# An encoder block on one core: conditioning sums by POOL products and accumulating DMAs, values split once, four mixer passes written out

## The reference

```
c_act = silu(c)
mod = c_act @ w_ada + b_ada          # (6*1024): sh1, sc1, g1, sh2, sc2, g2
h = rms_norm(x, norm1_gain) * (1 + sc1) + sh1
x = x + g1 * token_mixer(h, ...)
h = rms_norm(x, norm2_gain) * (1 + sc2) + sh2
x = x + g2 * conv_ffn(h, ...)
# token_mixer: one input projection to B, C, u | q, k, v | g_A, g_B
y_a = B * dwconv3(C * u)
y_b = windowed attention (|t-s| <= 128, 16 query heads, 4 key/value heads, ALiBi, sink)
merged = sigmoid(g_A) * y_a + sigmoid(g_B) * y_b ; out = merged @ w_o
```

## Time and profile before

| | us |
|---|---|
| median of 3 runs (870.09 to 871.1) | 870.67 |
| span of the profiled execution | 870.4 |
| the four mixer passes in it (72.5 to 168.3, 260.6, 350.4, 441.8) | 95.8, 92.3, 89.8, 91.4 |
| PE busy over the span | 799.9 (92%) |
| DVE busy over the span | 615.6 (71%) |
| POOL busy over the span | 377.8 (43%) |

### The profile page before, as it was taken

The page is one execution under the profiler, slowest core; times in us unless marked ns, Lnnn a source line. Parts: engine busy times, 40 slices in busy tenths (PEclk is TensorE's granted clock), DMA queues, the critical chain, the costliest instruction groups (busy, mean ns, idle before and its releaser), DMA issues.

```text
span 870.4 us, 11305 instructions
## 1 busy us (share of the span) xinstructions
PE 799.9 (92%) x3753; PEld 656.6 (75%) x3753; DVE 615.6 (71%) x781; ACT 349.3 (40%) x589; POOL 377.8 (43%) x170
## 2 busy tenths in 40 slices
PE   3579699998999899979999899999999999999997
PEld 2468577877777777867778788888888888887886
DVE  5969899598959996898753788888888888200000
ACT  5326245454345444534542454444444443122220
POOL 3824342443325243422494434555555555445341
PEclk9679799998999999999999999999999999999999
DMA  9813612362134413541123132232222322223311
GB/s 329 303 49 131 208 57 90 117 200 69 52 140 155 134 48 99 188 146 48 48 78 116 49 98 96 96 96 96 96 96 96 96 96 84 97 85 108 120 37 48
DMA packets 79726, 95.79 MB, mean 110 GB/s; under 512 B 2210, under 2 KB 71002, under 8 KB 79706
## 3 DMA queue, kind: packets, MB, share of 16 engines
q1 hardware_dynamic: 75482, 93.43, 32.2%
q10 hardware_dynamic: 4224, 2.10, 0.8%
HBM read 93.43 MB, written 2.10 MB: 110 GB/s over the span
## 4 chain that ended last, share of the span: by engine, by line
PE 64%; DVE 22%; issue 9%; DMA 3%; ACT 1%; DVEq 1%; SPq 0%; ACTq 0%
PE bank L652 20%; PE bank L654 20%; PE bank L653 20%; DVE acc L1083 2%; DVE a_buf L1173 2%; DVE prob L1124 2%; DMA ada<-in_w_ada_dram 2%; DVE sm L1140 1%; DVE acc L996 1%; DVE sm L1131 1%; PE bank L791 1%; PE bank L775 1%; DVE prob L1143 1%; DVE q_st L1096 1%; DVE pt_lo L1149 1%
## 5 line engine op out<-in xcount | busy, mean ns | idle before, releaser
L341 POOL TENSOR_TENSOR w_lo<-w_raw,w_hi 128x1024 fp32r<-128x1024 f32 x127 | 333.5, 2645 | 432.7 <-ACT w_hi L415 432.7
L652 PE MATMUL bank<-h_hi,w_hi 128*128 128x512 f32 (+1 forms) x792 | 310.5, 392 | 5.5 <-DVE h_lo L1317 4.3
L653 PE MATMUL bank<-h_lo,w_hi 128*128 128x512 f32 (+1 forms) x792 | 307.0, 388 | 0.0
L654 PE MATMUL bank<-h_hi,w_lo 128*128 128x512 f32 (+1 forms) x792 | 306.7, 387 | 0.0
L652 PEld LDWEIGHTS bank<-h_hi,w_hi 128*128 128x128 f32 x792 | 151.2, 191 | 36.2 <-DVE h_lo L1317 4.0
L654 PEld LDWEIGHTS bank<-h_hi,w_lo 128*128 128x128 f32 x792 | 151.0, 191 | 30.4
L653 PEld LDWEIGHTS bank<-h_lo,w_hi 128*128 128x128 f32 x792 | 151.1, 191 | 28.5
L415 ACT ACTIVATE w_hi<-w_raw 128x1024 fp32r<-128x1024 f32 x128 | 128.7, 1051 | 108.6 <-PE bank L654 102.0
L654 PE MATMUL bank<-g_hi,w_lo 128*128 128x512 f32 x176 | 70.0, 398 | 0.0
L652 PE MATMUL bank<-g_hi,w_hi 128*128 128x512 f32 x176 | 69.9, 397 | 0.0
L653 PE MATMUL bank<-g_lo,w_hi 128*128 128x512 f32 x176 | 69.3, 394 | 0.0
(11 more groups left out here) (175 smaller groups left out, 1076.5 us busy)
## 6 DMA issues: line engine op xcount, KB each, us to landing
w_raw<-in_w_in_dram SPq DMA_DIRECT2D x26, 1024.0 KB, 5.1
ada<-in_w_ada_dram SPq DMA_DIRECT2D x48, 512.0 KB, 6.0
w_raw<-in_w_up_dram SPq DMA_DIRECT2D x22, 1024.0 KB, 5.1
w_raw<-in_w_down_dram SPq DMA_DIRECT2D x8, 1024.0 KB, 4.9
w_raw<-in_w_o_dram SPq DMA_DIRECT2D x4, 1024.0 KB, 5.0
w_raw<-in_w_down_dram SPq DMA_DIRECT2D x4, 768.0 KB, 4.2
x_nat<-in_x_dram SPq DMA_DIRECT2D x4, 512.0 KB, 4.9
out_dram<-b_buf ACTq DMA_DIRECT2D x4, 256.0 KB, 2.3
```

What stands on the lines that cost most here:

```text
L341: pool.tensor_tensor(w_lo[:, n % 2, u], w_raw[:, n % 2, :, u * P:(u + 1) * P], w_hi[:, n % 2, u], SUB).then_inc(lo_ready, 1)
L652: pe.matmul(dst, w_h, rhs_hi, start=first, stop=False)
L653: pe.matmul(dst, w_h, rhs_lo, start=False, stop=False)
L654: return pe.matmul(dst, w_l, rhs_hi, start=False, stop=last)
```

## The change

The four passes are written out (`for g in range(KV)`) on all engines instead of looped. `v_nat` goes: ACT copies the high part of the values of all four heads straight from PSUM to a larger `v_st`, and DVE subtracts the low part, once, ahead of the passes. `gemv` leaves DVE. POOL makes each product of row block k in place (k = 0 goes straight to `acc`), and for k = 1 to 7 issues a DMA that adds the row to `acc` in SBUF; a DMA waits for the one before it. The steps stand one between the two halves of `low` and one behind. PE's `ada_turn` moves from slots 13 and 17 to slots 22 and 23, and DVE's `ada_sums` with it. SP's loads of `ada` now wait for a product or an accumulation instead of `gemv_done`; those of k = 0 and 1 for the last pass's `ada_turn` (`mod_done`).

```diff
-        v_nat = sb("v_nat", [P, NB, KV * HD], into=mixer)
-        v_st = sb("v_st", [P, NB, 2, HD], f32r, into=mixer)
+        v_st = sb("v_st", [P, NB, KV, 2, HD], f32r, into=mixer)
...
@@ sync
-                    for k in ([], [], [0, 1, 2, 3], [4, 5], [6, 7], [])[n]:
-                        sp.wait_ge(gemv_done, g * KT + (G0 + k - 1))
+                    for k in ([], [], [0, 1], [2, 3], [4, 5], [6, 7])[n]:
+                        if k < 2:
+                            sp.wait_ge(mod_done, g * 2 + 4)
+                        elif k == 2:
+                            sp.wait_ge(ada_scaled, g * KT + 1)
+                        else:
+                            sp.wait_ge(ada_added, g * (16 * (KT - 1)) + 16 * (k - 2))
...
@@ gpsimd
-            with pool.Fori(0, KV) as g:
+            for g in range(KV):
+                def ada_step(k):
+                    row = ada[:, k % 2, :]
+                    pool.wait_ge(ada_in[k % 2], g * (8 * KT) + (16 * (k // 2) + 16))
...
+                    pool.tensor_scalar(acc[:, :] if k == 0 else row, row, c_act[:, 0, k:k + 1], 1.0,
+                                       MUL, MUL).then_inc(ada_scaled, 1)
+                    if k == 0:
+                        return
+                    pool.wait_ge(ada_scaled, g * KT + (k + 1))
+                    if k > 1:
+                        pool.wait_ge(ada_added, g * (16 * (KT - 1)) + 16 * (k - 1))
+                    pool.dma_start(acc[:, :], row, accum_op=ADD).then_inc(ada_added, 16)
...
-                    low(g, NM, P_MIX + n + 1)
+                    low(g, NM, P_MIX + n + 1, (0,))
+                    if 1 <= n <= 4:
+                        ada_step(2 * n - 1)
+                    low(g, NM, P_MIX + n + 1, (1,))
+                    if n < 4:
+                        ada_step(2 * n)
@@ scalar
-            act.activation(v_nat[:, 2, :], bank[6][:, 0:PC], ACT.Copy).then_inc(o_free, 1)
+            for b in V_ORDER:
+                act.activation(v_st[:, b, :, 0, :], v_heads(b), ACT.Copy).then_inc(v_high, 1)
@@ tensor
-                    pe.wait_ge(gemv_done, g * KT + (G0 + KT))
+                    pe.wait_ge(ada_scaled, g * KT + KT)
+                    pe.wait_ge(ada_added, g * (16 * (KT - 1)) + 16 * (KT - 1))
...
-                    if slot in (13, 17):
-                        ada_turn((slot - 13) // 4)
+                    if slot in (22, 23):
+                        ada_turn(slot - 22)
@@ vector
-            for b, done in ((0, t_free), (1, t_free), (3, m_free)):
-                dve.tensor_copy(v_nat[:, b, :], bank[4 + b][:, 0:PC]).then_inc(done, 1)
+            for n, b in enumerate(V_ORDER):
+                dve.wait_ge(v_high, n + 1)
+                dve.tensor_tensor(v_st[:, b, :, 1, :], v_heads(b), v_st[:, b, :, 0, :],
+                                  SUB).then_inc((t_free, t_free, o_free, m_free)[b], 1)
...
-                gemv(0)
-                gemv(1)
-                stage_values()
                 query_low(0)
-                gemv(2)
-                gemv(3)
                 query_sums(0)
...
                 take(0, (0, 1))
-                gemv(4)
                 take(0, (2, 3))
-                gemv(5)
                 shift(0)
-                gemv(6)
-                gemv(7)
                 take(1, (0, 1))
```

More of the change, by code:

```diff
@@ L196, in encoder_block @@
         r_copy, xr_pool = sem("x_rstd_copied"), sem("x_normed_by_pool")
+        ada_scaled, ada_added = sem("ada_scaled"), sem("ada_added")
         cb_done, pe_ada, mod_read, amp_done = sem("c_spread"), sem("ada_used_by_pe"), sem("mod_read"), sem("amp_done")
@@ L231, in encoder_block, with v_heads @@
         WO_HALVES = [(0, 6, 6), (0, 7, 7), (1, 6, 4), (1, 7, 5)]
+        V_ORDER = (2, 3, 0, 1)
+        def v_heads(b):
+            return bank[4 + b][:, 0:PC].rearrange("p (j d) -> p j d", d=HD)
         def half(c):
@@ L262, in encoder_block @@
         NT = 10
-        STEPS, STEPS_UP = 36, 8
+        STEPS_UP = 8
         block = ctx.enter_context(nc.Block())
@@ L311, in _ @@
                     load(None, 0, 1, wi[:, :, COL_V:COL_V + PC])
-            with sp.Fori(1, KV + 1) as g1:
-                g = g1 - 1
+            for g in range(KV):
+                g1 = g + 1
                 for n in range(NM):
                     load(g, NM, P_MIX + n, wi[:, :, bass.ds(g1 * PC + (MIX[n] - PC), PC)])
-                    for k in ([], [], [0, 1, 2, 3], [4, 5], [6, 7], [])[n]:
-                        sp.wait_ge(gemv_done, g * KT + (G0 + k - 1))
+                    for k in ([], [], [0, 1], [2, 3], [4, 5], [6, 7])[n]:
[5 more added lines that the diff above has]
+                            sp.wait_ge(ada_added, g * (16 * (KT - 1)) + 16 * (k - 2))
                         sp.dma_start(ada[:, k % 2, :],
@@ L371, in _ @@
             low(None, 0, 2)
-            with pool.Fori(0, KV) as g:
+            pool.wait_ge(cb_done, 1)
+            for g in range(KV):
+                def ada_step(k):
+                    row = ada[:, k % 2, :]
+                    pool.wait_ge(ada_in[k % 2], g * (8 * KT) + (16 * (k // 2) + 16))
+                    if k == 0:
+                        pool.wait_ge(mod_done, g * 2 + 4)
+                    pool.tensor_scalar(acc[:, :] if k == 0 else row, row, c_act[:, 0, k:k + 1], 1.0,
+                                       MUL, MUL).then_inc(ada_scaled, 1)
+                    if k == 0:
+                        return
[3 more added lines that the diff above has]
+                    pool.dma_start(acc[:, :], row, accum_op=ADD).then_inc(ada_added, 16)
                 for n in range(NM):
@@ L468, in _ @@
                                    ACT.Copy).then_inc(kh_done, 1)
-            with act.Fori(0, KV) as g:
+            for g in range(KV):
                 U = 2 * P_MIX
@@ L729, in _ @@
                 mm.then_inc(kt_done, 1)
-            with pe.Fori(0, KV) as g:
+            for g in range(KV):
                 def unit_waits(n):
@@ L787, in values @@
                     last = i == len(TS[b]) - 1
-                    hi_lo = (bank[OB][:, :], v_st[:, kb], pt_hi[:, t % 2, :])
-                    hi = (bank[OB][0:HD, :], v_st[:, kb, 0, :], pt_lo[:, t % 2, :])
+                    hi_lo = (bank[OB][:, :], v_st[:, kb, g], pt_hi[:, t % 2, :])
+                    hi = (bank[OB][0:HD, :], v_st[:, kb, g, 0, :], pt_lo[:, t % 2, :])
                     for n, args in enumerate((hi, hi_lo) if last else (hi_lo, hi)):
@@ L1228, in _ @@
                 taps(1)
-                ada_sums(0)
                 conv_out(1)
@@ L1238, in _ @@
                 turned_low(TS[2][2:])
-                ada_sums(1)
                 normalise(3)
@@ L1243, in _ @@
                 turned_low(TS[3])
+                ada_sums(0)
                 heads_out(3)
+                ada_sums(1)
                 dve.wait_ge(m_free, g * 2 + 3)
@@ L1250, in _ @@
                 merge(1)
-                steps.leave(KV)
             steps.link(dve.scalar_tensor_tensor(amp[:, 1, :], mod[:, 4 * KT:5 * KT], 1.0, par[:, PA_G2:PA_G2 + KT],
```

3 lines of the change are left out of this document (1 added, 2 removed).

## The result

The changed kernel takes **890.9 us** (median of 4 runs, 880.4 to 902.2), beside 870.9 (870.1 to 874.8) for the kernel before. The ratio is 1.012 [1.0095, 1.0148], so the change makes the kernel slower, by 1.2%. The forecast was 841 (834 to 868) and faster. The time of the changed kernel is far more scattered than that of before; I read its profiled run, which took 884.5 us with a span of 882.7, against the span of 870.4 of before.

What follows compares the result with a forecast made beforehand. PE, busy 92% of the span, was taken to bound the kernel, with its waits ended by DVE. Passes of 86.5 + 3 x 84.4 = 339.7 us against 369.3 took 29.6 off, giving 841 us (834 to 868).

Steps and rivals of the forecast that it cites:

- (4): Eight products on POOL, 1.0 us each, 8 us a pass; nothing waits for them, holds of DVE about 1 us at most.
- (1): Eight conditioning steps leave DVE: waits for take go, 1.0 us of waits stays, passes 1 to 3 take 84.4 us each.
- (2): Pass 0: the 6.7 us wait for take goes, 0.6 and 0.7 stay; the pass becomes 86.5 us.
- (3): Values split once, ahead of pass 0: the way to the first query gets 0.8 us longer (0.4 to 1.2).
- U: Rival set up for the experiments: the written-out loops, the split of the values or the later ada_turn cost the time.
- (5): Seven accumulating DMAs in a chain, done before slot 22: free while each takes under 8.5 us; 42.7 us in all.
- A: Time of one accumulating DMA from its issue on POOL to landing, taken as 6.1 us (3.5 to 12.3).
- (6): Second low halves, SP's tile loads and the first ada rows stand behind new waits; all covered by existing room.
- (7): ada_turn at slots 22 and 23: same eight transposes, cost 0; writing out the loops gains 0 to 1 us a pass.
- The late chain: Rival: slot 22 waits for the accumulations, 883 us at 10 us per DMA, 947 at 12.3; chance 0.22.
- Held at the norm: Rival: POOL's work holds DVE's norm steps, take ends 2.5 us late before slot 7; 851 to 859 us, chance 0.15.

Runs made afterwards that it cites:

- e2: The changed kernel with all eight products on POOL but without the accumulating DMAs (sums wrong): 879.9 us, ratio 1.009.
- e1: The changed kernel without product and accumulating DMA for k = 1 to 7 (rows left out of the sums): 848.4 us, ratio 0.974.
- e5: The changed kernel with the products on ACT and POOL's DMAs before or behind a pair of low halves, computation whole: 848.7 us, ratio 0.973.
- e11: The changed kernel run again with no edit: 896.4 us (873.0 to 902.6), beside 871.3 for the kernel before.
- e4: The changed kernel with gemv back on DVE and the ada loads in their old places: 872.9 us, ratio 1.002.
- e10: e5 with the DMAs of k = 1, 4 and 6 issued between the two halves of a low: 861.5 us, ratio 0.988.

## Why the prediction was wrong

**The step that failed is (4), products on POOL**: "Nothing waits for them by themselves. Each is an interval more in which a DVE instruction can be held, about 1 us at most; DVE has 14.8 us more room." The sizes were nearly right: a product takes 1.13 us where it is alone (1.0 forecast), 1.2 on average, and a hold is 0.9 us a product (e2 less e1). What was wrong is that the sum got 0 for it, on account of DVE's room. Room is an average over a pass. The holds fall on DVE at the norm, at `normalise` and at the steps ahead of `take`, just where PE waits, and there they are paid, with slower matmuls behind them: 25.0 us of holds became 20.0 us of PE's waits and 10.3 more of its busy time, 31.5 us in all by the medians. Behind a pair of halves POOL used to pause, and a held step got through at the pair's end (so it still is in e5, 1.15 us); a product now fills the beginning of that pause, and the hold goes on through it, 4.15 us in pass 1.

The way from 841 to 882.4, by the runs: 841 forecast; 848.4 with neither product nor DMA, +7.4; products, +31.5; DMAs beside products, 882.4 - 879.9 = +2.5. The last can't be told from nothing: with the two shortest runs of e11 (874.6 in the middle) it is -5.3, and DMAs without products cost nothing. What makes six of the ten runs of the changed kernel take 894 to 903 us, no experiment shows.

**(1) Steps off DVE**: right, as e1 shows, where nothing else came in their place: the waits before PE's scores fall from 21.1 us to 3.5. A term of it was too small: I let 1.0 us of waits stay in a pass by halving those of L775 and L791. With `low` still holding `normalise`, PE's waits for that line alone are 7.1 us in e1, 11.8 in all against a forecast of 5.3; that is 6.5 of the 7.4.

**(2) Pass 0**: forecast 0.6 + 0.7 + 1.0 = 2.3 us of waits, measured 13.4, most of it by step (4): in e1, without the seven products, PE's waits up to 165 us are 2.2 + 1.7 + 0.3 = 4.2 us.

**(3) Values split once**: 0.8 forecast; pass 0 starts 0.9 later. With the rest of U it comes to 1.2 us in e4 (872.9 against 871.7), so no gain from writing out the loops shows.

**(5) The chain**: right that it is free. A was taken as 6.1, and the accumulations land after 6.1 in the median (4.6 to 10.8). That the two agree to a tenth is in part luck: the 5.1 in it is the load's time with no accumulation beside it, and beside them the same load takes 7.9; the 1 us for the descriptors had no row, and the nearest measured time is the 0.89 that an issue takes on POOL. In pass 1 the last accumulation is issued at 242.88 and PE comes to `ada_turn` at 261.78, 19 us later. The 4.4 of the Trainium skill ("DMA: Bandwidth & Descriptors", Anatomy of one DMA) is too low here; the measurement decides.

**(6) Queues moved past**: right. The 1 MB loads take 7.9 us instead of 5.1 beside the accumulations, and no PE wait in the passes is for them. **(7)**: right, no wait for `acc`.

**The rivals.** The late chain, to which I gave most of the slower cases, did not come. *Held at the norm* was the mechanism that came: 3.07 us at slot 7 where I worked out 2.5, with the slow clock behind it. Its time of 851 to 859 was too low because I priced one place in a pass. Of PE's 36.5 us of waits, 15.1 are for `take` (L797), 11.5 for `normalise` (L808) and 9.9 behind it (L823). An estimate with all three is 841 + 36.5 - 5.3 = 872, 5.3 being the waits already in the forecast, and the slow clock comes on top; the case belonged to the slower ones.

## What to carry to other kernels

When work moves from DVE to POOL, ask which of DVE's small steps PE waits for, and whether the new POOL instruction can lie on them; a hold there can cost PE most of its length (3.07 of 4.15 us in pass 1), however idle DVE is on average. The same products on ACT, with the DMAs still issued by POOL, make this kernel 2.7% faster than before (848.7 us, e5). And a rival that is a mechanism must be priced at every place where it can act, not at the first one found.

## What the runs showed of the hardware

- A DVE step of 0.18 us was held for 4.15 us, across the end of a DMA issue, a POOL TENSOR_TENSOR and the TENSOR_SCALAR behind it. In e2 one step got in between the two (2.27, then 1.05). When it does and when not stays open.
- A POOL memset lets DVE steps with two SBUF inputs through (0.17 us, eight of eight) and holds a TENSOR_SCALAR (0.87 us for 4 columns instead of 0.17; 1.17 us for 384 columns instead of 0.42).
- In e10 one DVE TENSOR_SCALAR of 384 columns took 3.32 to 3.35 us instead of 0.42 across a POOL TENSOR_TENSOR of 2.65 to 2.7 us, in each of eight groups.
- The issue of a DMA takes POOL 0.89 us and holds DVE by 0.14 us on average (3.9 us for 28).
- An accumulating DMA of 512 KB within SBUF takes 6.1 us from issue to landing in the median (4.6 to 10.8). Beside such DMAs loads of 1 MB take 7.9 us instead of 5.1.
